# Paged attention: VectorE turns half of the latent columns in 32 by 32 blocks, scored on sixteen tiles

## The chip, the cores and the metric

The kernel runs on one core of one Trainium2 chip. The metric is the device time of one execution in microseconds (us). A profiled execution gives a span (first to last instruction) and a trace of every engine: PE (TensorE matmuls), PEld (its weight loads), VectorE (DVE), ScalarE (ACT), GpSimd (POOL) and SyncE (SP).

## What is computed

The reference is one step of a decoder layer for a prompt of 512 tokens and for 8 sequences with 4 new tokens each, over a paged cache of 4096 past positions per sequence. The part that matters here is the attention of the new tokens (8 heads, 32 queries per sequence in all) over the cache, in which each position is a row of 256 latent and 32 rope numbers:

```python
past = cache_l[page_table].reshape(Bd, -1, KV_CACHE_DIM)
q_lat = jnp.einsum('bthd,chd->bthc', q_nope, lp["w_uk"])          # absorption
s_past = einsum('bthc,bkc->bhtk', q_lat, pc) + einsum('bthr,bkr->bhtk', q_rope, pr)
p = softmax(concat(s_past, masked s_new) * MLA_SCALE)
ctx = einsum('bhtk,bkc->bthc', p[..., :n_past], pc) + einsum(..., p[..., n_past:], nc)
```

In front of it stands causal attention over the prompt (8 heads, blocks of 128 queries), behind it the output projection, cross-attention to a memory and an MLP. All of it is f32; the large projections are done as three fp32r products of high and low parts.

## The kernel before

Every engine has a program of its own, ordered by hand; semaphores tie them together. Stages, on PE: projections (`act_tile`, L582), prompt attention (L870 to L916), the paged loop (L976 to L999), then output projection, memory attention and MLP.

**Prompt attention** is a software pipeline over n = 0 to 36 (32 pairs of head and query block): PE makes the score of n (L885), VectorE adds the causal mask and takes the maximum (L1943, L1944), ScalarE the exp (L1518), VectorE scales by the reciprocal (L1949, L1950), PE turns p of n - 3 (L893), ScalarE copies it (L1526), PE multiplies by the values of n - 5 (L907). Between these, `k_pair` (three times inside the loop, at n = 3, 11, 17) makes two heads' keys. The **absorption** runs in the gaps: `absorb_turn` (n = 18, 20, 22, 24; L839) transposes w_uk, ScalarE copies it (L1537), `absorb` (n = 27, L847) makes 16 products of a 64 by 128 weight with 32 columns, VectorE copies the result into `qlat` by head (L1928). `new_rows` (n = 30, L858 to L863) scores the new tokens' own rows, with three waits of PE on itself between products of different tiling. VectorE spreads the rope queries into `qropez` (L1918), block-diagonal, which POOL has set to zero (L540).

**The paged loop.** One turn handles 2048 positions (half of a sequence), 16 in all. POOL gathers them by indirect DMA into one of four buffers `pg` (L526), 128 partitions by 16 positions by 288 numbers, as soon as the values of four turns ago are done. PE's order in turn n is `turn(n+1)`, `turn_p(n)`, `score(n+1)`, `values(n)`:

- `turn` (L929): 32 transposes of 128 by 128, four to a PSUM bank, four banks of `gps` in rotation; ScalarE (L1549) and VectorE (L1965) copy the banks alternately to `cT`.
- `score`: with the queries' latents as weights of 32 columns, on four column tiles (32j), 8 products of 512 columns (L943) and 16 rope products of 128 columns against `qropez` (L949), into `aux` bank 1 or 2.
- VectorE takes the maximum (L1981) and its negative (L1982), turns the rope part of the next page in 32 by 32 blocks (L1970); ScalarE makes exp with the sum (L1562).
- `turn_p` (L960): four transposes of p, copied by VectorE to `pTs` (L1990). `values` (L970): 16 products of 256 columns on four column tiles into `aux` bank 3, kept by ScalarE (L1553).

POOL's queue in this stage: the zeroing of `qropez` behind the last key tile, `gather(1)` behind the last `absorb_turn`, `gather(2)` behind `absorb`, `gather(3)` behind the last `at_lo`, then `gather(i+4)` behind `values(i)`; the split of the output weights stands behind all of them. The loop on PE:

```python
for n in range(NH - 1):
    turn(n + 1); turn_p(n); score(n + 1); values(n)
```

## Time and profile before

| | us |
|---|---|
| median of 3 runs | 1029.64 (1028.56 to 1030.25) |
| profiled execution: its own time | 1030.06 |
| its span | 1028.3 |
| busy: PE / PEld / VectorE / ScalarE / POOL | 996.3 / 900.5 / 515.4 / 300.4 / 447.5 |
| prompt attention, first score to first page transpose | 203.8 to 265.8 |
| paged loop, first turn with copies done to last exp | 274.8 to 402.5 |

The span is the stretch between the first and last instruction; 1.8 us of the execution lie around it. PE's ends are modelled, so a busy PE is one with work in its pipeline; start-to-start times tell what an instruction costs.

### The profile page before, as it was taken

What the parts mean: (1) busy time and instruction counts of PE and PEld (TensorE: products, weight loads), DVE (VectorE), ACT (ScalarE), POOL (GpSimd) and SP (SyncE); (2) the same over time, 40 slices, a digit from 0 to 9 for tenths busy, and PEclk for the clock granted to TensorE, in tenths of its full rate; (3) what the DMA queues carried; (4) which work ended last, traced back from release to release, by engine and by line L of the source; (5) the groups of instructions that cost most, each with busy time, mean ns of one, the idle gap of its engine ahead of it and who ended that gap; (6) DMA issues with size and microseconds to landing.
All of it is one profiled execution on the core that took longest, in us unless ns stands there. A gap on an engine that the chain in (4) does not pass through costs nothing.

```text
span 1028.3 us, 19824 instructions
## 1 busy us (share of the span) xinstructions
PE 996.3 (97%) x8517; PEld 900.5 (88%) x8517; DVE 515.4 (50%) x723; ACT 300.4 (29%) x602; POOL 447.5 (44%) x284
## 2 busy tenths in 40 slices
PE   5999999999999999999999999999999999999997
PEld 5989898766677777999965799999999999999997
DVE  5789998377455555563255366421341134114413
ACT  7333265475344443121035122210120022002222
POOL 4545688500011112555320155555555555555551
PEclk9999999998999999999999999999999999999998
DMA  7323365503377772822192022233223322332222
GB/s 227 84 67 81 104 184 153 169 32 152 147 274 278 278 279 80 270 83 82 61 404 90 21 83 83 82 94 92 82 83 91 94 83 83 93 93 83 83 82 87
DMA packets 140556, 130.39 MB, mean 127 GB/s; under 512 B 13477, under 2 KB 133170, under 8 KB 136630
## 3 DMA queue, kind: packets, MB, share of 16 engines
q1 hardware_dynamic: 134888, 88.55, 28.4%
q0 software_dynamic: 2304, 37.75, 9.5%
q10 hardware_dynamic: 3278, 2.83, 0.8%
q8 instruction: 67, 1.10, 0.4%
q14 instruction: 19, 0.16, 0.0%
HBM read 123.53 MB, written 5.03 MB: 125 GB/s over the span
## 4 chain that ended last, share of the span: by engine, by line
PE 84%; DVE 8%; ACT 2%; POOL 2%; DMA 2%; issue 2%; SPq 0%; ACTq 0%; DVEq 0%; POOLq 0%
PE gps L582 56%; PE gps L929 5%; PE aux L943 3%; PE aux L970 3%; PE aux L885 1%; PE gps L1085 1%; PE gps L1167 1%; PE aux L949 1%; PE gps L907 1%; POOL wlo L521 1%; PE gps L736 1%; PE gps L1005 1%; DVE act_lo L1681 1%; PE gps L718 1%; PE aux L1098 1%
## 5 line engine op out<-in xcount | busy, mean ns | idle before, releaser
L582 PE MATMUL gps<-act_hi,whi 128*128 128x272 f32 x912 | 265.8, 291 | 5.8 <-POOL wlo L511 3.4
L497 POOL TENSOR_SCALAR whi<-wraw 128x1024 fp32r<-128x1024 f32 (+1 forms) x109 | 114.6, 1052 | 360.1 <-PE gps L582 298.8
L582 PE MATMUL gps<-act_lo,whi 128*128 128x272 f32 x912 | 264.2, 290 | 0.0
L582 PE MATMUL gps<-act_hi,wlo 128*128 128x272 f32 x912 | 263.8, 289 | 0.0
L500 POOL TENSOR_TENSOR wlo<-wraw,whi 128x1024 fp32r<-128x1024 f32 (+1 forms) x109 | 257.5, 2363 | 9.1
L582 PE MATMUL gps<-h_hi,whi 128*128 128x272 f32 x640 | 185.7, 290 | 0.0
L582 PE MATMUL gps<-h_lo,whi 128*128 128x272 f32 x640 | 185.1, 289 | 0.0
L582 PE MATMUL gps<-h_hi,wlo 128*128 128x272 f32 x640 | 184.6, 288 | 0.0
L582 PEld LDWEIGHTS gps<-act_hi,whi 128*128 128x128 f32 x912 | 172.4, 189 | 6.9 <-issue 3.9
L582 PEld LDWEIGHTS gps<-act_hi,wlo 128*128 128x128 f32 x912 | 172.4, 189 | 0.3 <-issue 0.2
L582 PEld LDWEIGHTS gps<-act_lo,whi 128*128 128x128 f32 x912 | 172.3, 189 | 0.0
L2024 DVE TENSOR_TENSOR XT<-gps,XT 128x544 f32<-128x544 f32 x48 | 34.8, 724 | 174.3 <-PE gps L582 171.7
L582 PEld LDWEIGHTS gps<-h_hi,whi 128*128 128x128 f32 x640 | 120.5, 188 | 0.4
L582 PEld LDWEIGHTS gps<-h_hi,wlo 128*128 128x128 f32 x640 | 120.5, 188 | 0.1
L582 PEld LDWEIGHTS gps<-h_lo,whi 128*128 128x128 f32 x640 | 120.4, 188 | 0.0
L1630 ACT ACTIVATE ms<-mr 128x544 f32<-128x544 f32 x32 | 21.1, 660 | 287.2 <-DVE mr L2105 287.2
L2111 DVE TENSOR_TENSOR act_lo<-ms,act_hi 128x544 fp32r<-128x544 f32 x29 | 58.5, 2017 | 40.8 <-ACT act_hi L1634 40.8
L526 POOL DMA_INDIRECT pg<-in_cache_mla_dram,idx x16 | 15.2, 953 | 134.0 <-PE aux L970 99.2
L929 PEld LDWEIGHTS gps<-ident,pg 128*128 128x128 f32 x512 | 55.5, 141 | 8.1 <-issue 5.9
L929 PE MATMUL gps<-ident,pg 128*128 128x128 f32 x512 | 60.0, 275 | 1.1 <-DVE ctxn L1978 0.8
L1965 DVE COPY cT<-gps 128x512 f32<-128x512 f32 x64 | 44.1, 690 | 25.9 <-PE gps L929 25.8
L2105 DVE SCALAR_TENSOR_TENSOR mr<-gps,rsn 128x544 f32<-128x544 f32 x32 | 23.2, 725 | 65.4 <-PE gps L582 64.6
(367 smaller groups left out, 1539.0 us busy)
## 6 DMA issues: line engine op xcount, KB each, us to landing
wraw<-in_w_up_dram SPq DMA_DIRECT2D x32, 512.0 KB, 4.0
wraw<-in_w_down_dram SPq DMA_DIRECT2D x32, 512.0 KB, 3.7
wraw<-in_w_in_dram SPq DMA_DIRECT2D x14, 512.0 KB, 4.2
kv<-in_cache_mem_k_dram SPq DMA_DIRECT2D x7, 1024.0 KB, 7.0
kv<-in_cache_mem_v_dram SPq DMA_DIRECT2D x7, 1024.0 KB, 13.0
wraw<-in_w_mem_k_dram SPq DMA_DIRECT2D x16, 256.0 KB, 2.9
wraw<-in_w_mem_v_dram SPq DMA_DIRECT2D x16, 256.0 KB, 3.2
wraw<-in_w_out_dram SPq DMA_DIRECT2D x8, 512.0 KB, 4.7
```

The costliest lines, as they stand in the source:

```text
L497: nc.gpsimd.tensor_scalar(whi[:, slot, 0:n], wraw[:, slot, 0:n], 1.0, 1.0, ALU.mult, ALU.mult).then_inc(pool_step, 1)
L500: nc.gpsimd.tensor_tensor(wlo[:, slot, 0:n], wraw[:, slot, 0:n], whi[:, slot, 0:n].bitcast(F32), ALU.subtract).then_inc(w_ready, 1)
L526: nc.gpsimd.indirect_dma_start(pg[n % 4][:, :, :].rearrange("p k d -> p (k d)"), None, rows_of_pages, bass.IndirectOffsetOnAxis(ap=idx[:, ...
L582: mm = nc.tensor.matmul(out_of(a), w_of(w, k), x_of(x, k, part), start=(k == 0 and s == 0), stop=(k == k_tiles - 1 and s == 2))
L929: mm = nc.tensor.transpose(gps[:, (k + 1) % 4, 128 * z:128 * z + 128], pg[n % 4][:, 4 * j + z, 128 * c:128 * c + 128], ident[:, :])
L943: nc.tensor.matmul(out[32 * j:32 * j + 32, :], qlat[:, c, b, :], cT[:, c, 512 * j:512 * j + 512], start=(c == 0), stop=False, skip_group_c ...
L970: mm = nc.tensor.matmul(aux[32 * j:32 * j + 32, 3, 0:256], pTs[:, 128 * i + 32 * j:128 * i + 32 * j + 32], pg[n % 4][:, 4 * j + i, 0:CR], ...
L1630: nc.scalar.activation(ms[:, n % 2, :], mr[:, n % 2, :], ACT.Square).then_inc(mlp_sq, 1)
L1965: V.tensor_copy(cT[:, i // 4, 512 * (i % 4):512 * (i % 4) + 512], gps[:, (k + 1) % 4, :]).then_inc(g_td, 1)
L2024: step(V.tensor_tensor(x, gps[:, 2 * (t % 2):2 * (t % 2) + 2, 0:HALF], x, ALU.add))
L2105: V.scalar_tensor_tensor(out=halves(mr[:, n % 2, :]), in0=gps[:, 2 * (t % 2):2 * (t % 2) + 2, 0:HALF], scalar=0.0, in1=halves(rsn[:, :]), ...
L2111: V.tensor_tensor(hidden(n)[1], ms[:, n % 2, :], hidden(n)[0].bitcast(F32), ALU.subtract).then_inc(mlp_lo, 1)
```

## The change

- Of a page's 256 latent columns, PE transposes the first 128 only, in two parts (`turn(n, part)`), through two banks of `aux`, all copied by ScalarE. The other 128 VectorE turns in 32 by 32 blocks, four stream transposes per page straight from `pg` to `cB`, with no PSUM between.
- Within such a block only 32 latent numbers lie on 32 partitions, so the second half and the rope are scored as 5 x 4 x 4 products of 32 rows, 32 columns of weights and 128 moving columns, on all sixteen tiles, each row group into its own bank of `gps`. The first half is added by 16 products on four column tiles. Scores have one set of banks, read by one reduce and one exp over four banks. `qropez` is replaced by `qB` (the second half's queries, in four blocks of 32) and `qrope4`.
- `values(n-1)` stands between the two parts of `turn(n+1)`.
- The absorption is turned: w_uk's transposes stand at the start of prompt attention and are copied by VectorE; the product has q as the weights (32 columns) and w_uk as 256 moving columns; its result is copied, spread four times and transposed back in three rounds (`absorb_back`, `block_back`). `new_rows` takes rope and mask in one product of 96 rows, without waits on itself.
- POOL's zeroing goes; `gather(2)` waits for the last round of turning back.

```diff
-        qropez = at("qropez", [128, BD, 128], F32, M0 + 46016)
+        qB = at("qB", [128, BD, 4, 32], F32, M0 + 46016)
+        qrope4 = at("qrope4", [128, BD, 32], F32, M0 + 39936)
...
-                    nc.gpsimd.memset(qropez[:, :, :], 0.0).then_inc(pool_set, 1)
                     pool.wait_ge(wk_T, 4)
                     gather(1)
-                    pool.wait_ge(ql_ps, 1)
+                    pool.wait_ge(ql_ps, 4)
...
             def absorb_turn(g):
 
-                if g == 0:
-                    pe.wait_ge(tile_free[1], (T_UK + 3) // 2 + 1)
-                else:
-                    pe.wait_ge(wk_ev, g)
+                if g >= 2:
+                    pe.wait_ge(wk_ev, 2)
                 for i in range(4):
                     h, c = 2 * g + i // 2, i % 2
                     o = 512 * c + 64 * h
-                    mm = nc.tensor.transpose(W_BANK[0:64, 128 * i:128 * i + 128], wraw[:, U_UK % 2, o:o + 64], ident[:, :])
+                    mm = nc.tensor.transpose(gps[0:64, (1, 3, 2, 3)[g], 128 * i:128 * i + 128],
+                                             wraw[:, U_UK % 2, o:o + 64], ident[:, :])
                 mm.then_inc(wk_T, 1)
 
             def absorb():
 
                 pe.wait_ge(wk_ev, 4)
-                for h in range(H):
-                    for c in range(2):
-                        mm = nc.tensor.matmul(W_BANK[:, (c * H + h) * TS:(c * H + h + 1) * TS],
-                                              wukT[:, h, 128 * c:128 * c + 128], q[0:64, h, TP:T],
-                                              start=True, stop=True)
+                pe.wait_ge(tile_free[1], (T_UK + 3) // 2 + 1)
+                for g in range(2):
+                    for h in range(4):
+                        mm = nc.tensor.matmul(W_BANK[32 * h:32 * h + 32, CR * g:CR * g + CR], q[0:64, 4 * g + h, TP:T],
+                                              wukT[:, 4 * g + h, :], start=True, stop=True, skip_group_check=True)
                 mm.then_inc(ql_ps, 1)
 
+            def absorb_back():
+
+                pe.wait_ge(ql_ok, 1)
+                for c in range(2):
+                    for g in range(2):
+                        o = 256 * c + 128 * g
+                        mm = nc.tensor.transpose(W_BANK[:, o:o + 128], qln[:, g, 128 * c:128 * c + 128], ident[:, :])
+                mm.then_inc(ql_ps, 1)
+
+            def block_back(p):
+
+                pe.wait_ge(ql_ok, 2 + p)
+                for x in range(2):
+                    for g in range(2):
+                        o = 256 * x + 128 * g
+                        mm = nc.tensor.transpose(W_BANK[:, o:o + 128],
+                                                 qlr[:, g, 2 * p + x, :, :].rearrange("p r d -> p (r d)"), ident[:, :])
+                mm.then_inc(ql_ps, 1)
+
...
-                    nc.tensor.matmul(out, qrc[64:96, 128 * g:128 * g + 128], kr[64:96, TP:T], start=False, stop=False
-                                     ).then_inc(new_row, 1)
-                    pe.wait_ge(new_row, 2 * g + 1)
-                    mm = nc.tensor.matmul(out, newmask[0:TS, 4 * g:4 * g + 4, :].rearrange("p b q -> p (b q)"),
-                                          ident[0:TS, 0:TS], start=False, stop=True)
-                    if g == 0:
-                        mm.then_inc(new_row, 1)
-                        pe.wait_ge(new_row, 2)
+                    mm = nc.tensor.matmul(out, qrc[0:96, 128 * g:128 * g + 128], kr[0:96, TP:T], start=False, stop=True)
...
+            absorb_turn(0)
+            absorb_turn(1)
...
-                    if n in (3, 11, 17):
-                        k_pair(n // 8 + 1)
+                    if n == 3:
+                        absorb_turn(2)
+                        absorb_turn(3)
+                    if n == 4:
+                        pe.wait_ge(wk_ev, 3)
+                        k_pair(1)
+                    if n in (11, 15):
+                        k_pair((n + 1) // 5)
...
-                if 18 <= n <= 24 and n % 2 == 0:
-                    absorb_turn((n - 18) // 2)
-                if n == 27:
+                if n == 18:
                     absorb()
+                if n == 22:
+                    absorb_back()
+                if n in (25, 28):
+                    block_back((n - 25) // 3)
                 if n == 30:
...
-            def turn(n):
-
-                pe.wait_ge(page_in[n % 4], 16 * (n // 4) + 16)
-                for i in range(8):
-                    k = 8 * n + i
-                    if k >= 4:
-                        pe.wait_ge((g_ta, g_td)[k % 2], (k - 4) // 2 + 1)
+            def turn(n, part):
+
+                if part == 0:
+                    pe.wait_ge(page_in[n % 4], 16 * (n // 4) + 16)
+                for i in (2 * part, 2 * part + 1):
+                    k = 4 * n + i
+                    if k >= 2:
+                        pe.wait_ge(g_ta, k - 1)
                     else:
-                        pe.wait_ge((at_pT, new_act, at_lo, at_lo)[k], (4 * H, 2, 3, 4)[k])
+                        pe.wait_ge(at_exp, 4 * H)
                     for z in range(4):
-                        c, j = divmod(i, 4)
-                        mm = nc.tensor.transpose(gps[:, (k + 1) % 4, 128 * z:128 * z + 128],
-                                                 pg[n % 4][:, 4 * j + z, 128 * c:128 * c + 128], ident[:, :])
+                        mm = nc.tensor.transpose(aux[:, 1 + k % 2, 128 * z:128 * z + 128],
+                                                 pg[n % 4][:, 4 * i + z, 0:128], ident[:, :])
                     mm.then_inc(g_T, 1)
 
             def score(n):
 
                 b = n // 2
-                out = aux[:, 1 + n % 2, :]
-                if n >= 2:
-                    pe.wait_ge(g_exp, n - 1)
-                for c in range(2):
-                    for j in range(4):
-                        k = 8 * n + 4 * c + j
-                        pe.wait_ge((g_ta, g_td)[k % 2], k // 2 + 1)
-                        nc.tensor.matmul(out[32 * j:32 * j + 32, :], qlat[:, c, b, :],
-                                         cT[:, c, 512 * j:512 * j + 512], start=(c == 0), stop=False,
-                                         skip_group_check=True)
+                if n == 0:
+                    pe.wait_ge(at_pT, 4 * H)
+                    pe.wait_ge(new_act, 2)
+                    pe.wait_ge(at_lo, 4)
                 pe.wait_ge(g_rope, n + 1)
+                pe.wait_ge(g_td, 4 * n + 4)
+                for x in range(5):
+                    for g in range(4):
+                        rows = slice(32 * g, 32 * g + 32)
+                        for j in range(4):
+                            q_x, k_x = ((qB[rows, b, x, :], cB[rows, 4 * j:4 * j + 4, 32 * x:32 * x + 32]) if x < 4
+                                        else (qrope4[rows, b, :], ropT[rows, 4 * j:4 * j + 4, :]))
+                            nc.tensor.matmul(gps[32 * j:32 * j + 32, g, 0:128], q_x, k_x, start=(x == 0), stop=False,
+                                             skip_group_check=True)
+                pe.wait_ge(g_ta, 4 * n + 4)
                 for g in range(4):
                     for j in range(4):
                         mm = nc.tensor.matmul(
-                            out[32 * j:32 * j + 32, :].rearrange("p (i g k) -> p g i k", i=4, g=4)[:, g, :, :],
-                            qropez[:, b, 32 * g:32 * g + 32], ropT[:, 4 * j:4 * j + 4, :], start=False, stop=(g == 3),
-                            skip_group_check=True)
+                            gps[32 * j:32 * j + 32, g, 0:128], qlat[:, 0, b, :],
+                            cT[:, 512 * j:512 * j + 512].rearrange("p (i g k) -> p g i k", i=4, g=4)[:, g, :, :],
+                            start=False, stop=True, skip_group_check=True)
                 mm.then_inc(g_S, 1)
 
...
-                turn(n + 1)
+                turn(n + 1, 0)
+                if n:
+                    values(n - 1)
+                turn(n + 1, 1)
                 turn_p(n)
                 score(n + 1)
-                values(n)
...
-            def turned(n):
-                for k in range(8 * n, 8 * n + 8, 2):
+            def turned(n, part):
+                for k in (4 * n + 2 * part, 4 * n + 2 * part + 1):
                     act.wait_ge(g_T, k + 1)
-                    i = k % 8
-                    nc.scalar.copy(cT[:, i // 4, 512 * (i % 4):512 * (i % 4) + 512], gps[:, (k + 1) % 4, :]).then_inc(g_ta, 1)
+                    nc.scalar.copy(cT[:, 512 * (k % 4):512 * (k % 4) + 512], aux[:, 1 + k % 2, :]).then_inc(g_ta, 1)
 
...
-                nc.scalar.activation(ps[n % 2][:, :], aux[:, 1 + n % 2, :], ACT.Exp, bias=nm[:, n:n + 1],
-                                     scale=1.0, accum_out=sl[:, 1, n % 2, n // 2:n // 2 + 1]).then_inc(g_exp, 1)
+                nc.scalar.activation(ps[n % 2][:, :].rearrange("p (i g k) -> p g i k", i=4, g=4),
+                                     gps[:, :, 0:128].rearrange("p g (i k) -> p g i k", i=4), ACT.Exp,
+                                     bias=nm[:, n:n + 1], scale=1.0,
+                                     accum_out=sl[:, 1, n % 2, n // 2:n // 2 + 1]).then_inc(g_exp, 1)
+                if n < NH - 1:
+                    turned(n + 1, 0)
                 if n >= 1:
                     keep_ctx(n - 1)
                 if n < NH - 1:
-                    turned(n + 1)
+                    turned(n + 1, 1)
...
+            def spread(r):
+
+                src = gps[:, 2, :].rearrange("p (g c) -> p g c", g=2)[:, :, 128:256]
+                return V.tensor_copy(qlr[:, :, :, r, :], src.rearrange("p g (x d) -> p g x d", x=4))
+
+            def by_head(dst, x):
+
+                return V.tensor_copy(dst.rearrange("p b (h t) -> p h b t", t=TD),
+                                     gps[:, 2, x * 256:x * 256 + 256].rearrange("p (h b t) -> p h b t", h=H, t=TD))
+
             def absorbed(n):
 
                 if n == 18:
                     dve.wait_ge(tile_done, T_UK + 4)
-                    dve.wait_ge(pool_set, 9)
-                elif n < 23:
-                    if n == 19:
-                        dve.wait_ge(q_ok, 16 * H)
-                    r = 32 * (n - 19)
-                    step(V.tensor_copy(qropez[r:r + 32, :, r:r + 32].rearrange("p b (h t) -> p h b t", t=TD),
-                                       q[R, :, TP:T].rearrange("p h (b t) -> p h b t", t=TD)))
+                    dve.wait_ge(q_ok, 16 * H)
+                elif n == 19:
+                    dve.wait_ge(ql_ps, 1)
+                    V.tensor_copy(qln[:, :, :], gps[:, 2, :].rearrange("p (g c) -> p g c", g=2))
+                    spread(0)
+                elif n == 20:
+                    spread(1)
+                    spread(2)
+                elif n == 21:
+                    spread(3).then_inc(ql_ok, 1)
                 elif n == 23:
+                    dve.wait_ge(ql_ps, 2)
+                    by_head(qlat[:, 0, :, :], 0)
+                    by_head(qlat[:, 1, :, :], 1).then_inc(ql_ok, 1)
+                elif n in (26, 29):
+                    p = (n - 26) // 3
+                    dve.wait_ge(ql_ps, 3 + p)
+                    by_head(qB[:, :, 2 * p, :], 0)
+                    by_head(qB[:, :, 2 * p + 1, :], 1).then_inc(ql_ok, 1)
+                elif n == 24:
+                    V.memset(qrc[32:64, :], 0.0)
+                    V.memset(kr[32:64, TP:T], 0.0)
+                    V.tensor_copy(qrc[0:32, :].rearrange("p (b q) -> p b q", b=BD), newmask[:, :, :])
+                    V.tensor_copy(kr[0:32, TP:T], ident[0:32, 0:32])
                     step(V.tensor_copy(qrc[R, :].rearrange("p (b h t) -> p h b t", b=BD, t=TD),
                                        q[R, :, TP:T].rearrange("p h (b t) -> p h b t", t=TD)))
-                elif n == 24:
+                elif n == 27:
                     step(V.tensor_reduce(pick[:, :], ident[:, :].rearrange("p (j q) -> p q j", j=4), AX, ALU.add))
-                elif n == 28:
-                    dve.wait_ge(ql_ps, 1)
-                    for c in range(2):
-                        ins = V.tensor_copy(qlat[:, c, :, :].rearrange("p b (h t) -> p h b t", t=TD),
-                                            gps[:, 2, c * 256:c * 256 + 256].rearrange("p (h b t) -> p h b t", h=H, t=TD))
-                        if c == 0:
-                            step(ins)
-                    ins.then_inc(ql_ok, 1)
-                elif n == 32:
+                elif n == 31:
                     dve.wait_ge(new_pe, 1)
                     step(V.tensor_reduce(sn[:, 0, :], gps[:, 2, 0:64].rearrange("p (g k) -> p g k", g=2), AX, ALU.max))
                     V.tensor_scalar(nmn[:, :], sn[:, 0, :], -1.0, None, ALU.mult).then_inc(new_dve, 1)
-
+                elif n in (33, 34):
+                    for r in (64 * (n - 33), 64 * (n - 33) + 32):
+                        V.tensor_copy(qrope4[r:r + 32, :, :].rearrange("p b (h t) -> p h b t", t=TD),
+                                      q[R, :, TP:T].rearrange("p h (b t) -> p h b t", t=TD))
+
+            def turned_uk(g):
+
+                dve.wait_ge(wk_T, g + 1)
+                V.tensor_copy(wukT[:, 2 * g:2 * g + 2, :],
+                              gps[0:64, (1, 3, 2, 3)[g], :].rearrange("p (h n) -> p h n", h=2)).then_inc(wk_ev, 1)
+
+            turned_uk(0)
+            turned_uk(1)
...
+                if n == 2:
+                    turned_uk(2)
+                    turned_uk(3)
...
-                for k in range(8 * n + 1, 8 * n + 8, 2):
-                    dve.wait_ge(g_T, k + 1)
-                    i = k % 8
-                    V.tensor_copy(cT[:, i // 4, 512 * (i % 4):512 * (i % 4) + 512], gps[:, (k + 1) % 4, :]).then_inc(g_td, 1)
+                for j in range(0, 16, 4):
+                    V.transpose(cB[:, j:j + 4, :], pg[n % 4][:, j:j + 4, 128:256]).then_inc(g_td, 1)
...
-                step(V.tensor_reduce(sl[:, 0, n % 2, n // 2:n // 2 + 1], aux[:, 1 + n % 2, :], AX, ALU.max))
+                step(V.tensor_reduce(sl[:, 0, n % 2, n // 2:n // 2 + 1], gps[:, :, 0:128],
+                                     mybir.AxisListType.XY, ALU.max))
```

## Rows read from the trace of the kernel before

**Rows 1.** The page, the chain that ended last: shares of the span by engine.

```profile
PE 84%; DVE 8%; ACT 2%; POOL 2%; DMA 2%; issue 2%; SPq 0%; ACTq 0%; DVEq 0%; POOLq 0%
```

**Rows 2.** Windows: us, busy us (instructions) by engine, clock granted, DMA share, GB/s.

```profile
203.80:247.30 43.50, 39.77 (x270) 26.81 (x270) 35.23 (x114) 30.23 (x89) 1.90 (x2) 1.00 0.13 51
247.30:265.80 18.50, 18.16 (x118) 14.39 (x118) 8.06 (x28) 7.16 (x26) 0.94 (x1) 0.72 0.57 228
...
274.80:402.50 127.70, 127.51 (x1732) 93.35 (x1736) 72.98 (x122) 51.85 (x104) 14.97 (x15) 1.00 0.62 235
```

**Rows 3.** The chain through one turn of the loop: start us, us, what.

```profile
335.00 3.64 PE gps L929 x32
338.65 0.44 PE aux L960 x4
339.08 1.85 PE aux L943 x16
340.94 0.87 PE aux L949 x32
341.81 1.73 PE aux L970 x32
343.54 0.26 PE gps L929
```

**Rows 4.** Weight loads in the same turn, in order of time.

```profile
334.93 3.47 PEld L929 LDWEIGHTS gps<-ident,pg 128*128 128x128 f32 x32 [0.41 <-issue]
...
339.01 0.16 PEld L943 LDWEIGHTS aux<-cT,qlat 128*32 128x32 f32 x8 [0.17 <-issue]
```

**Rows 5.** Groups of instructions, 283.8 to 402.5: count, busy us, mean ns, idle before.

```profile
L1965 DVE COPY cT<-gps 128x512 f32<-128x512 f32 x56 | 38.7, 692 | 24.7 <-PE gps L929 24.7
L1549 ACT COPY cT<-gps 128x512 f32<-128x512 f32 x56 | 32.8, 586 | 14.6 <-PE gps L929 14.6
...
L1981 DVE TENSOR_REDUCE sl<-aux 128x1 f32<-128x512 f32 x14 | 9.7, 692 | 26.7 <-PE aux L949 26.7
L1990 DVE COPY pTs<-aux 128x512 f32<-128x512 f32 x14 | 9.5, 680 | 0.0
L1970 DVE STREAM_TRANSPOSE ropT<-pg 128x512 f32<-128x512 f32 x13 | 9.1, 701 | 0.0
L1562 ACT ACTIVATE ps<-aux,nm 128x512 f32<-128x512 f32 x13 | 8.9, 687 | 51.5 <-DVE nm L1982 51.5
...
L943 PEld LDWEIGHTS aux<-cT,qlat 128*32 128x32 f32 x224 | 5.8, 109 | 10.7 <-issue 10.7
```

**Rows 6.** PE at the query rope swap, on 32 by 32 tiles: start, us.

```profile
183.72 1.12 PE L776 MATMUL aux<-qr,swap 32*32 32x272 f32 x16
```

**Rows 7.** The page gathers: one issue on POOL's timeline, and all sixteen landings.

```profile
335.31 0.94 POOL L526 DMA_INDIRECT pg<-in_cache_mla_dram,idx  x1 [7.59 <-PE aux L970]
...
DMA to landing us min/median/max: 8.4/9.5/11.0
```

**Rows 8.** The page, DMA queues: packets, MB, share of 16 engines.

```profile
q0 software_dynamic: 2304, 37.75, 9.5%
```

**Rows 9.** The chain at the absorption, and VectorE before two later scores.

```profile
247.33 3.69 PE gps L847 x32
...
252.10 0.30 DVE L1943 TENSOR_TENSOR aux<-aux,causal 128x128 f32<-128x128 f32 x1 [3.06 <-PE aux L885]
...
261.36 0.30 DVE L1943 TENSOR_TENSOR aux<-aux,causal 128x128 f32<-128x128 f32 x1 [4.49 <-PE aux L885]
```

**Rows 10.** VectorE in prompt attention, 204.5 to 263.4, groups as in rows 5.

```profile
L1918 DVE COPY qropez<-q 32x256 f32<-32x256 f32 x4 | 1.1, 284 | 0.1
L1928 DVE COPY qlat<-gps 128x256 f32<-128x256 f32 x2 | 0.8, 421 | 0.0
```

**Rows 11.** Windows in late prompt attention, columns as in rows 2.

```profile
251.00:254.00 3.00, 3.00 (x12) 1.97 (x12) 1.80 (x6) 0.94 (x3) 0.94 (x1) 0.52 0.51 154
...
261.00:265.80 4.80, 4.63 (x36) 3.23 (x37) 2.20 (x9) 1.97 (x10) 0.00 (x0) 0.64 0.01 2
```

35 lines of the change are left out of this document (19 added, 16 removed).

## The prediction

> **What bounds the kernel now.** I read the chain that ended last first: 84% of it is TensorE [rows 1]. Then the windows by stage [rows 2]: prompt attention, 203.8 to 265.8 us, and the paged loop, 274.8 to 402.5 us, hold nearly all that the change touches. In the loop PE is busy in 127.51 of 127.70 us; in the first 43.5 us of prompt attention VectorE is busy in 35.23 and PE in 39.77. The rest of the kernel, projections and MLP, keeps its code.
>
> One turn of the loop [rows 3]: 32 transposes of the page 3.64 us, 4 of p 0.44, the latent score 1.85, the rope score 0.87, the values 1.73; sum 8.53, and the next turn begins at 343.54, 8.54 after 335.00. Nobody makes PE wait: the idle time in front of the copies on both helpers is put down to PE [rows 5]. So in the loop the time is PE's instruction list, 15 turns of 8.53.
>
> How small matmuls cost: each f32 matmul is two instructions. A transpose takes 3.64/32 = 0.114 with its share of a change of tiling; without it 0.109, the 0.44/4 of p's. The rope score, 16 matmuls of 128 columns on four column tiles, is 32 instructions in 0.87, 0.027 each: four run side by side, one wave per 0.109. Eight weight loads of four tiles fit into 0.16 us at 109 ns each [rows 4, 5], so loads follow each other by (0.16 - 0.109)/7 = 7 ns when their tiles are free. Sixteen tiles at 7 ns would be 0.11 us, just a wave.
>
> **The loop after.** PE per turn:
> 1. Page transposes: 16 instead of 32, 16 x 0.109 = 1.75 (saved 1.75).
> 2. p's four, unchanged, 0.44. Values, unchanged, 1.73.
> 3. First latent half: it was half of 1.85, 0.93; now 16 matmuls of 128 columns on four column tiles in four banks, the same form as the old rope score: 0.87.
> 4. Second half and rope: 80 matmuls of 32 by 32 with 128 columns, 160 instructions. The only 32-by-32 tiling with long streams is the query rope swap [rows 6]: 16 instructions of 272 columns in 1.12; a stream is 272/128 x 0.109 = 0.23, and four waves of four at 0.23 and the last one's drain fill just that: tiles that differ in row and column run together, but no row shows several row groups in one column group. The bounds: all sixteen in parallel, 10 waves x 0.109 = 1.09; row groups one after another, 40 x 0.109 = 4.37. I take 1.09: loads and matmuls of parked tiles are passed by others already (all four tiles start within 0.03 us although each tile's two passes stand together in the list), and the four banks keep the row groups' outputs apart. It replaces 0.93 + 0.87.
> 5. Changes of tiling. Two per turn show as gaps of the weight loads, 0.41 and 0.17 us [rows 4]; the delay in them is 8.53 less the streams, (32 + 4) x 0.109 + 16 x 0.109 (512 columns on four tiles) + 0.87 + 1.73, which leaves 0.26; I take 0.15 each. The new order (transposes, values, transposes, p, sixteen tiles, four tiles) has five: 0.75.
>
> Sum 1.75 + 0.44 + 1.73 + 0.87 + 1.09 + 0.75 = 6.63 us.
>
> Does another engine reach that? VectorE loses four copies of 0.69 and gains four stream transposes of 512 elements, 0.70 like the rope's [rows 5]: with reduce 0.69, negation 0.15, rope 0.70, p's copy 0.68 it has 5.0 of 6.6. Its order: reduce, negation, rope turn, four turns (about 4.2 after a score's end), while PE comes to the next score after 1.75 + 1.73 + 0.44 and four changes, 4.5. Near, but PE last. ScalarE keeps four copies of 0.59 and an exp. The single set of score banks is safe: reduce, negation and exp take 0.69 + 0.15 + 0.69 + 0.2, 1.8 with hand-overs, and PE has 3.9 of other work before it needs them. The p copy waits for p's transposes and hides beside the next score, since values now come a turn later.
>
> Pages: a gather takes 9.5 us from issue to landing, 0.94 of them on POOL [rows 7], and one turn's page is 37.75/16 = 2.36 MB; the queue's 9.5% of the span is 97.7/16 = 6.1 us a page with all sixteen DMA engines [rows 8]. So DMA alone allows 6.1. The gather of page n+4 waits for values n, which moved from the end of turn n to 2.9 us into turn n+1; with 0.5 for the hand-over (334.9 to the issue at 335.31) it lands 3.4 + 9.5 = 12.9 after that turn's start and is needed two turns on: a turn of 6.45 is allowed. Close below 6.63; for small waits where both are near I take **6.7**.
>
> Total of the stage: turn 0 has no values, but two of its copies stand behind the first exp: about 6.2. Then 14 x 6.7, and the last values outside the loop, 1.85: 101.9, against 15 x 8.53 = 128.0 and about 0.3 of first-turn waits. **Saved 26.4.**
>
> **Prompt attention.** The absorption was 32 instructions in 3.69 with VectorE idle 3.06 [rows 9]; turned it is 16 instructions of 256 columns on four tiles, 16/4 x 0.22 = 0.9. Three rounds of transposing back add 12 x 0.109 and six changes of tiling, 2.2. The new rows lose two mask products and the waits between them; VectorE waited 4.49 there; about 1.5 to 2 stays. Against that stands VectorE, which paces this part. Added inside it: two of the four weight copies moved from ScalarE (0.69; the first two lie before the first score, where it idles, but delay it by some 0.4), one 512 copy 0.69, four spreads and four more by-head copies at 0.42, the mask pieces for the joint product about 0.7, less four rope copies of 0.28 that go behind the last score [rows 10]: 1.3 + 0.7 + 3.4 + 0.7 - 1.1 + 0.4 = 5.4. Removed idle time: 2 + 2.7. ScalarE sheds 4 x 0.59, PE no longer stands for it in the weight turns. The clock fell to 0.52 at 251 and 0.64 in the last stretch [rows 11], each after sparse 32-column streams; losing one of these stretches gives back 1 to 2 us. Net: -0.5, between -5 and +4. The moved gathers (the second no longer behind the memset, the third behind the last turning back) have landed long before their turn; the waits on POOL's queue cost nothing, as the weight split behind them waits for the stage's end anyway. Start of the stage: the first score waits for VectorE's subtraction, rope turn and four turns, some 4.6 us, as it now starts 4.4 in: nothing.
>
> Sum against the profiled execution's 1030.06: - 26.4 - 0.5 = **1003**; it lies 0.4 above the median of 1029.64, which changes nothing.
>
> The Trainium skill, "TensorE: Matmul & The Clock Gate", Part 3, says that matmuls keep strict program order in start and end. By that rule, taken literally, the two passes of each of the 80 products would stand 0.109 apart one after the other: 8.7 us a turn and a kernel of over 1100. This trace disagrees already: 16 such products on four tiles take 0.87, not 1.75. The same page gives 10.6 times for sixteen tiles, which no row here shows.
>
> **Rivals.**
> - **A tile's second pass holds the next row group.** Within a column group the list reads first pass, second pass, next row group. If a column's queue stays in order, each of the 20 steps costs 0.109 + 0.007 to 0.027: 2.3 to 2.7, a turn of 7.85 to 8.25, the stage 119 to 125: 1020 to 1027, middle 1022. For it: no row has this case. Against: queues that let other tiles past. Chance 0.16. This is also the case that the tiling is not what it says.
> - **Gathers late.** Landing took up to 11.0 [rows 7]; now two are in flight. Then a turn is (3.4 + 11)/2 = 7.2, the stage 109: 1010. Chance 0.12.
> - **Row groups share a column's path.** The 160 instructions take 4.37, the turn 9.9: turn 0 9.5 + 14 x 9.9 + 1.85 = 150, 22 more: 1051. It decides against the change from 1.09 + 1.9 = 3.0 us for the 160. Chance 0.12.
> - Forecast, 0.6, its own range 997 to 1009.
>
> Numbers: 1003; the range 996 to 1023 leaves out the last rival and the upper end of the first. A measurement of this kernel tells 0.2%, 2 us, from no change. The top of the first rival with 2 or 3 us more in prompt attention is no change: faster 0.86, same 0.02, slower 0.12.
>
> **What would show it.** Loop turns of 6.6 to 6.8 in the chain, PE still without waits; the 160 small matmuls spanning about 1.1 us a turn. 2.3 to 2.7 or 4.4 there is the first or last rival; a wait of PE or VectorE for a page's DMA at turn starts is the second. VectorE waits of less than 2 us around absorption and new rows, prompt attention within 4 us of 62. Wrong altogether if the clock falls inside the loop, or if a change of tiling costs much more than 0.15.

## The result and the profile after

| | before | after |
|---|---|---|
| median of 4 runs, us | 1029.33 (1028.56 to 1030.25) | 1079.61 (1078.28 to 1082.92) |
| profiled span, us | 1028.3 | 1078.8 |
| first score of prompt attention to first page transpose | 62.0 | 59.5 |
| from there to the start of the loop | 9.0 | 12.4 |
| loop, 15 turns | 127.7 | 177.8 |
| from the loop's end to the end of the span | 625.8 | 625.6 |

The changed kernel is slower, 1.05 times the time of before (95% interval 1.0482 to 1.0518). The forecast was 1003 us, with a range of 996 to 1023. The table puts the whole loss into the loop: 50.1 of 50.5 us.

The windows of the changed kernel by stage: us, busy us (instructions) by engine, clock granted, DMA share, GB/s. They answer to [rows 2].

```profile
203.60:247.30 43.70, 39.64 (x265) 26.50 (x266) 34.69 (x109) 26.28 (x78) 0.94 (x1) 0.96 0.22 89
247.30:263.00 15.70, 13.02 (x108) 8.82 (x106) 13.86 (x50) 9.21 (x32) 0.94 (x1) 1.00 0.40 151
263.00:275.40 12.40, 8.31 (x216) 6.08 (x214) 4.78 (x10) 2.73 (x5) 0.94 (x1) 0.84 0.57 237
275.40:453.20 177.80, 139.02 (x3656) 101.14 (x3660) 68.64 (x122) 48.30 (x105) 18.00 (x16) 0.86 0.44 168
```

The last line is the loop. PE, busy without a break before, is busy in 139.02 of 177.80 us, and its clock, 1.00 before, is granted at 0.86 on average: part of the time it is at the lower of its two levels, 1.2 GHz instead of 2.4. No other engine is near its limit, and DMA moves less than before (168 GB/s for 235). The number of PE's instructions is in the same line: 3656 matmuls where the loop had 1732.

What does PE wait for? The waits of PE in the loop: what it stood in front of, the releaser, us in total, how often, the longest.

```profile
PE gps L975 <- issue: 17.7, 8, 4.9
PE gps L980 <- issue: 11.4, 3, 4.4
PE aux L1001 <- issue: 6.1, 3, 2.2
PE aux L956 <- issue: 3.3, 1, 3.3
```

"issue" means that no semaphore, engine or transfer known to the profile held it: 38.5 us of nothing. In the chain that ended last "issue" rose from 2% [rows 1] to 5%. The stops are long, few, and in four different places of the code (the small products, the first-half products, the values, the transposes), so they don't belong to one instruction. PE's timeline around one of them, start, us, what, idle before:

```profile
349.34 1.64 PE L975 MATMUL gps<-cB,qB 32*32 32x128 f32 x102
...
350.83 0.67 PE L975 MATMUL gps<-ropT,qrope 32*32 32x128 f32 x28
351.43 0.41 PE L980 MATMUL gps<-cT,qlat 128*32 128x128 f32 x5
355.55 0.87 PE L980 MATMUL gps<-cT,qlat 128*32 128x128 f32 x12 [3.70 <-issue]
```

The first line starts with the window; its group began at 349.18. PE stops after five of a row of 32 like instructions. Windows cut from one resumption to the next show the pattern:

```profile
316.60:341.00 24.40, 18.77 (x511) 13.29 (x511) 9.05 (x16) 6.38 (x14) 1.87 (x2) 0.85 0.52 198
341.00:355.60 14.60, 10.90 (x258) 7.62 (x261) 4.53 (x8) 3.19 (x7) 0.94 (x1) 0.73 0.42 161
355.60:370.30 14.70, 10.34 (x258) 7.60 (x261) 4.53 (x8) 3.19 (x7) 0.94 (x1) 0.85 0.43 165
```

About 256 matmuls and as many weight loads lie in each. Counted in the trace itself, with PE's semaphore instructions, it is 1024 instructions in the first window and 511 to 513 in each of the others, these two and the ones behind them: twice 256. The page has a DMA queue for instructions; its lines for the kernel before and, second, the changed one (packets, MB, share):

```profile
q8 instruction: 67, 1.10, 0.4%
```

```profile
q8 instruction: 83, 1.36, 0.5%
```

A packet is 16,384 bytes, 256 instructions of 64; I call these 256 a block. PE's 21,420 recorded instructions divided by 83 are 258: the queue feeds PE. In the records of the packets, each stop ends 1.2 to 1.6 us after one of them has landed. Every second block is on time, every second one is late, since a turn has two blocks (488 instructions and some waits, 232 before) and the sixteen-tile products run through most of one of them in 2 us:

```
changed kernel, counted from the stops in steps of 256 instructions
block entered   next packet runs      next block entered   PE idle before it
334.22          338.64 to 339.54      340.97               4.85
340.97          342.01 to 342.95      349.66               0
349.66          353.16 to 354.10      355.55               3.70
355.55          357.08 to 358.00      363.59               0
363.59          367.87 to 368.81      370.25               4.36
```

In the loop the packet mostly starts 0.8 to 1.9 us after a block is entered when the DMA engines are free, and 3.5 to 4.4 after it when a gather is running. The DMA share and the bytes of one gather, 333 to 342 us, in 40 slices (it was issued on POOL at 332.18):

```profile
DMA  0009970029939939937937977977991000100000
q0 software_dynamic: 144, 2.36, 68.7%
q8 instruction: 1, 0.02, 0.6%
```

One instruction packet among 128 gather packets of 18,432 bytes (and 16 small ones). That is theory F; the experiments try it.

It need not be a gather. The loop's last stop (4.14 us idle, ended at 448.66) follows the last gather: the block entered at 441.42 had its next packet only 4.73 us later, and 7.24 us passed to the next block. The DMA engines were busy with the output weights, in 2028 packets of some 510 bytes, 441.4 to 446.1 us:

```profile
q1 hardware_dynamic: 2028, 1.03, 78.0%
```

### The profile page after: what moved, and what is told of

It is laid out like the page before. It is cut to its first block, busy times and chain, and to the rows that moved or that the text cites. A ratio compares the mean times of both kernels' runs of the same rounds, so it can differ in the third digit from the quotient of the medians.

```text
span 1078.8 us, 23919 instructions
## 1 busy us (share of the span) xinstructions
PE 1001.2 (93%) x10557; PEld 902.0 (84%) x10557; DVE 516.9 (48%) x740; ACT 293.9 (27%) x598; POOL 446.0 (41%) x283
## 4 chain that ended last, share of the span: by engine, by line
PE 78%; DVE 9%; issue 5%; POOL 2%; ACT 2%; DMA 2%; SPq 0%; ACTq 0%; DVEq 0%; POOLq 0%
PE gps L584 53%; PE gps L975 4%; PE aux L956 3%; PE aux L1001 3%; PE gps L980 2%; PE gps L1119 1%; POOL wlo L524 1%; PE gps L1201 1%; PE gps L1040 1%; DVE act_lo L1714 1%; PE gps L720 1%; DVE sm L2007 1%; DMA wraw<-in_w_mem_v_dram 1%; PE aux L991 1%; PE aux L1132 1%
## 5 line engine op out<-in xcount | busy, mean ns | idle before, releaser
L524 POOL TENSOR_TENSOR wlo<-wraw,whi 128x512 fp32r<-128x512 f32 x32 | 48.8, 1557 | 12.9 <-ACT whi L1363 12.9
L2045 DVE TENSOR_REDUCE sl<-gps 128x1 f32<-128x512 f32 x16 | 11.1, 691 | 78.0 <-PE gps L980 78.0
L1714 DVE SCALAR_TENSOR_TENSOR h_lo<-XT,vec,h_hi 128x544 fp32r<-128x544 f32 x16 | 40.5, 2533 | 15.6 <-ACT h_hi L1293 15.6
```

Source lines behind the costliest of these rows:

```text
L524: ins = nc.gpsimd.tensor_tensor(wlo[:, slot, part], wraw[:, slot, part], whi[:, slot, part].bitcast(F32), ALU.subtract)
L1714: V.scalar_tensor_tensor(out=lo, in0=XT[:, k, :], scalar=cols(gain, k), in1=hi.bitcast(F32), op0=ALU.mult, op1=ALU.subtract).then_inc(nx_l ...
```

## The experiments

Theories: **F**, the instruction block comes late because its packet waits among the gather's. **R1**, it comes late by its own latency, now that a turn has twice the instructions. **R2**, the stops are the sixteen tiles' own. Except in the last experiment each kernel was run once; before, run beside them, took 1027.6 to 1029.6 us.

### No gathers in the loop (e1_four_gathers)

```diff
-                    for i in range(NH - 4):
-                        pool.wait_ge(g_V, i + 1)
-                        gather(i + 4)
```

> The changed kernel with only the first four page gathers of sixteen; the later row groups read the four page buffers again, so what is computed for them is wrong data at the same cost. Theory F (TensorE stands still at every second block of 256 instructions, because the block's fetch, a 16,384 B packet, is queued on a DMA engine behind the gather's 18,432 B packets): the 2 to 5 us gaps of the loop disappear as soon as no gather runs, the granted clock of the loop stays near 1.0, a turn takes 7.2 to 8.2 us, and the kernel 1010 to 1032 us. Rival R1 (the fetch is late by its own latency, since a turn now has twice the instructions; gathers don't matter): gaps stay, 1065 to 1080 us. Rival R2 (the gaps are the sixteen-tile products' own, no matter of fetches): gaps stay, 1065 to 1080 us.

Measured: 1034.42 us. The loop, and two windows between resumptions:

```profile
299.40:308.70 9.30, 7.89 (x254) 5.85 (x254) 4.53 (x8) 3.19 (x7) 0.00 (x0) 1.00 0.01 4
308.70:318.00 9.30, 9.29 (x254) 7.00 (x254) 4.53 (x8) 3.19 (x7) 0.00 (x0) 0.82 0.02 4
265.40:404.90 139.50, 124.29 (x3812) 93.76 (x3816) 69.60 (x124) 47.57 (x104) 0.13 (x1) 0.96 0.08 29
```

And one stop, on PE's timeline:

```profile
306.99 0.30 PE L972 MATMUL gps<-ropT,qrope 32*32 32x128 f32 x3
308.71 0.71 PE L972 MATMUL gps<-ropT,qrope 32*32 32x128 f32 x25 [1.43 <-issue]
```

45 of the 50 us are gone with the gathers, so most of it is F. But the stops did not disappear, they shrank to 1.84 us and less, again 512 instructions apart: R1 holds for the rest. With idle DMA engines the packet typically starts 1.0 us after a block is entered, ends at 2.0 and opens the next block at some 3.4 us (2.9 to 3.5 in seven cases, 4.1 and 4.7 in two). A block that PE runs through faster than that stops it in any case. A turn is 139.5/15 = 9.3 us, still above before's 8.53, and above the 7.2 to 8.2 that F gave; the time, too, is 2 us over F's range.

The kernel before with the same lines removed is the control.

> The kernel before with only the first four gathers of sixteen (later row groups compute on old pages). Theory F: its 232 instructions a turn need one block of 256 in over 8 us, more than the 6.7 us that a fetch beside a gather took at most in the changed kernel, so that nothing is gained: 1025 to 1031 us, and no gaps in the loop. If the gathers cost the loop something else (TensorE reading more slowly beside them), it is faster by more than that: 1020 us or less.

Measured: 1028.83 us, before beside it 1027.58. The gathers cost it nothing.

### Twice the instructions in the kernel before (e4_before_split, e5_before_split_four_gathers)

```diff
-                        nc.tensor.matmul(out[32 * j:32 * j + 32, :], qlat[:, c, b, :],
+                        for s in range(4):
+                            nc.tensor.matmul(out[32 * j:32 * j + 32, 128 * s:128 * s + 128], qlat[:, c, b, :],
...
-                        mm = nc.tensor.matmul(aux[32 * j:32 * j + 32, 3, 0:256],
+                        for s in (0, 128):
+                            mm = nc.tensor.matmul(aux[32 * j:32 * j + 32, 3, s:s + 128],
```

The rope products are cut in two in the same way. The pieces begin their sums in a bank that others have begun, so the sums are not the reference's.

> The kernel before with its first score products cut into four of 128 columns, its rope products into two of 64 and its value products into two of 128: the same columns and the same four tiles, but 228 pairs of instructions a turn where it has 116, near the changed kernel's 244. Theories F and R1 (instruction fetch): gaps of 2 to 5 us appear in a kernel without sixteen tiles, they end 512 instructions apart, the turn grows by the 112 small pairs (some 1.5 us) and by the gaps (some 3 us), 1070 to 1105 us. Rival R2 (the gaps belong to sixteen tiles): no gaps, only the pairs: 1035 to 1055 us.

> The split kernel of the run before it, with only the first four gathers of sixteen (later row groups compute on old pages). Theory F: no gaps any more, the small pairs' own time is left: 1035 to 1055 us. R1: like the split kernel with all gathers, gaps included, within 10 us.

Measured: 1068.86 with all gathers, 1066.43 with four. The loop with all gathers, PE's only waits for "issue" in it, and then the loop with four:

```profile
274.00:438.00 164.00, 162.50 (x3274) 155.85 (x3276) 72.09 (x120) 51.80 (x104) 14.03 (x14) 1.00 0.48 182
```

```profile
PE aux L973 <- issue: 1.3, 3, 0.6
```

```profile
274.00:438.00 164.00, 163.34 (x3373) 157.81 (x3377) 72.69 (x122) 51.80 (x104) 5.21 (x4) 1.00 0.03 9
```

The first time lies between what was expected of F and R1 (1070 and more) and of R2 (1055 at most), and the stops of 2 to 5 us did not come: a kernel with nearly the changed kernel's count has three short ones and no more. The second is near the first, the number that R1 gave, but not for its reason, as there are no stops in it. The 40 us are the 112 extra pairs' own time: 39.6/16 = 2.5 us a turn, 22 ns a pair. The count alone is harmless because it is spread: from one block of 256 to the next pass mostly 4.4 to 9 us, and where it is less (2.7 to 3.3, three times) the packet came early. What counts is how fast a block is used up.

### Fewer small products (e3_two_of_five, e15_three_of_five)

```diff
-                for x in range(5):
+                for x in (0, 4):
```

> The changed kernel with only 32 of its 80 small score products (the second, third and fourth 32 latent columns of the second half are left out of the scores; VectorE still turns them): 296 instructions a turn instead of 488, still in sixteen tiles. Theory F: 1.2 blocks a turn at some 6.3 us beside a gather are 7.4 us, so hardly a gap is left and the turn is 7.5 to 8.1 us: 1018 to 1035 us. R2 (the gaps belong to sixteen tiles, whose products are still there): at most the time of the products left out is saved, 1.2 us a turn: 1055 to 1065 us.

> The changed kernel with 48 of its 80 small score products (the third and fourth 32 latent columns of the second half are left out of the scores): 360 instructions a turn, between the 296 of the run with 32 products and the 488 of the whole. Theory F (time goes by the number of blocks of 256 instructions): 1.45 blocks a turn at some 6.4 us are 9.3 us a turn, kernel 1035 to 1052 us. A share of the products' own time alone (0.4 us for each 32 columns): 1060 us or more; if the loss needs all five rounds of products (a matter of one burst's length): 1010 to 1018 us.

Measured: 1007.03 with 32 small products a turn, 1024.86 with 48, 1079.6 with 80. The loop with 32, and its "issue" waits:

```profile
265.00:380.00 115.00, 107.47 (x2339) 76.13 (x2339) 71.84 (x129) 49.23 (x109) 13.51 (x15) 0.96 0.74 283
```

```profile
PE aux L1001 <- issue: 2.3, 2, 1.6
PE gps L980 <- issue: 1.2, 2, 0.8
```

R2 falls: sixteen tiles are there in both, and a turn takes 7.0 us (first small product of the second turn to that of the last, over 14). Both runs came out below what F gave. I had put every block at 6.3 us; blocks entered outside a gather are faster, so the loss grows more steeply than the count. 16 products of 13 ns a pair are 0.4 us a turn, 6.6 us in all; the first sixteen left out bring some 27 us each (54.7 for two), the next 17.8. The difference is the stops and the clock.

### One pass instead of two (e8_single_pass)

```diff
+                            q_x, k_x = (a.bitcast(mybir.dt.bfloat16) for a in (q_x, k_x))
-                            nc.tensor.matmul(gps[32 * j:32 * j + 32, g, 0:128], q_x, k_x, start=(x == 0), stop=False,
+                            nc.tensor.matmul(gps[32 * j:32 * j + 32, g, 0:128], q_x[:, 1::2], k_x[:, :, 1::2], start=(x == 0), stop=False,
```

> The changed kernel with its small score products on the upper halves of the same numbers (read as 16-bit floats, so less exact), which makes one pair of instructions of each product instead of two: 80 products in the same sixteen tiles, 328 instructions a turn instead of 488. Theory F: 1.3 blocks a turn at some 6.3 us are 8.1 us, the turn is 7.6 to 8.6 us and the kernel 1020 to 1045 us, with shorter and fewer gaps. R2: 16-tile gaps stay, only the 1 us of the halved products goes: 1060 us or more.

Measured: 1016.47 us. All 80 products in all sixteen tiles, at half their instructions: 11 us faster than before, and again a few us below what F gave. R2 is out for good. It is no version to keep, as it scores half of the latent columns and the rope from 16 bits. Stops remain, up to 2.9 us (9.5 us in front of the values), and from one block to the next beside a gather passed 5.8 to 7.0 us.

### Smaller packets, and gathers at another time

The gather in four (or two) parts reads a quarter (half) of each row's bytes, with an index table for each part:

```diff
+                for s in range(4):
                     nc.gpsimd.indirect_dma_start(
-                    pg[n % 4][:, :, :].rearrange("p k d -> p (k d)"), None, rows_of_pages,
-                    bass.IndirectOffsetOnAxis(ap=idx[:, n:n + 1], axis=0)).then_inc(page_in[n % 4], 16)
+                        pg[n % 4][:, 4 * s:4 * s + 4, :].rearrange("p k d -> p (k d)"), None, rows_of_parts,
+                        bass.IndirectOffsetOnAxis(ap=idp[:, s, n:n + 1], axis=0)).then_inc(page_in[n % 4], 16)
```

> The changed kernel with every gather cut into four of a quarter of the bytes each (4,608 B a packet instead of 18,432), everything computed as before. F, if the fetch waits for packets that are already under way or takes turns with the gather's: smaller packets let it in sooner, gaps shrink by half or more, 1030 to 1055 us. F, if the whole backlog of the gather on that DMA engine is ahead of the fetch: gaps stay as the bytes do, 1070 to 1085 us. R1 and R2: no change, 1075 to 1085 us. GpSimd issues four times as many gathers; if their preparation takes long, pages come late and the turn grows, 1085 us or more.

Measured: 1062.79 us, 17 us better than the whole gathers. The late blocks beside a gather now took 4.1 to 6.3 us, most of them 5.3 or less, where they took 5.8 to 6.7. The packet gets in sooner. That it is the size of the gather's packets that lets it in is not shown by this: the four issues are also spread, 1.25 us apart.

> The changed kernel with every gather in two of half the bytes (9,216 B a packet). Theory F with the fetch taking its turn among the gather's packets: between the whole gather (1079.6 us) and the quarters (1062.8 us), 1064 to 1075 us, with block times between 6.5 and 4.6 us. If the quarters had gained by something other than the size of a packet (when they start), it is at one end or the other.

Measured: 1081.91 us, no gain at all: late blocks of 5.7 to 6.6 us but for one, and two new pauses, of some 0.3 and 0.56 us, inside the small products of most turns. That is the upper end of the second case, so packet size alone does not explain what the quarters gained; neither would it explain the 4.73 us beside packets of 510 bytes.

A gather issued behind the small products:

```diff
                         pool.wait_ge(g_V, i + 1)
+                        pool.wait_ge(g_S, i + 3)
```

> The changed kernel with every gather from the fifth on issued behind the small score products of the turn instead of ahead of them (one wait more on GpSimd; everything computed as before). Theory F: the block whose instructions run fastest, that of the small products, is then fetched with the DMA engines free (3.4 us from the block before to it, as in the run with four gathers), only the other one of a turn lies beside the gather (some 6.5 us): 9.9 us a turn where it was 10.9, kernel 1050 to 1068 us; if the gathers only slide until they meet the next dense block again, 1070 to 1082 us. If the gaps have to do with how late the pages come, it gets slower: 1085 us or more.

Measured: 1070.52 us, at the lower edge of the second case; eight stops of 2.2 to 4.4 us were left and had slid to other places of the turn, and PE waited twice for a page, 6.7 us in all. Both together:

> Both together: quarters, and issued behind the small products. Theory F: the dense block is fetched in some 3.4 us, the other in some 4.6 us, and the small products no longer run beside GpSimd's four issues (they took 2.6 us where they take 2.05 otherwise): 1035 to 1052 us. If the position of the gather doesn't matter: 1060 to 1065 us, as with the quarters alone.

Measured: 1077.56 us, a miss: worse than the quarters alone. PE waits for pages here too, 6.0 us.

> The single-pass kernel with every gather in four of a quarter of the bytes (4,608 B a packet). Theory F: both cures together, 1.3 blocks a turn at 4.6 us are 6.0 us, so the fetches are hidden and the gathers' own 7.6 us a page or TensorE's work bounds the turn: 1010 to 1028 us, at or below the kernel before. Otherwise within 5 us of the single-pass kernel.

Measured: 1070.3 us, the plainest miss of the study, 54 us above the same kernel with whole gathers. PE's groups in its loop:

```profile
L978 PE MATMUL gps<-cB,qB 32*32 32x128 bf16 x1024 | 26.9, 230 | 37.7 <-issue 35.7 <-DVE cB L2035 1.9
```

And one turn's small products on PE's timeline:

```profile
333.40 0.54 PE L978 MATMUL gps<-cB,qB 32*32 32x128 bf16 x41
334.36 0.26 PE L978 MATMUL gps<-cB,qB 32*32 32x128 bf16 x5 [0.42 <-issue]
335.09 0.27 PE L978 MATMUL gps<-cB,qB 32*32 32x128 bf16 x6 [0.46 <-issue]
336.52 0.26 PE L978 MATMUL gps<-cB,qB 32*32 32x128 bf16 x4 [1.16 <-issue]
```

These are not block ends: starts stand 0.68 us or twice that apart, and the 80 products take 4.7 us instead of 0.65 in twelve of the sixteen turns, all of them with a divided gather being issued.

> The single-pass kernel with quarters, issued behind the small products. In the same kernel with the issues ahead, the 80 small products took 4.7 us a turn instead of 0.65, in pauses of 0.68 us, while GpSimd prepared its four gathers. Theory P (the preparation of a gather on GpSimd holds up the small products): they take 0.65 us again, 1005 to 1020 us. Rival (the running gather's small packets hold them up, whenever they were issued, or where the data lie): they still take over 3 us in most turns, 1050 to 1075 us.

Measured: 1047.08 us. The 80 products take 0.65 us in nine of sixteen turns and 1.4 to 2.8 in seven; in addition PE now waits for pages, which start too late:

```profile
L959 PE MATMUL aux<-ident,pg 128*128 128x128 f32 x248 | 41.0, 318 | 20.6 <-DMA pg<-in_cache_mla_dram,idp 19.4 <-DVE ctxn L2049 0.8 <-ACT cT L1581 0.4
```

Neither side's numbers were met. What makes the 0.68 us pauses stays open: they came only with divided gathers, and moving the issues away thinned them without ending them. The f32 products with quarters have no such pause, but in the turns without a stop they take 2.5 to 3.0 us, mostly 2.6, instead of 2.05.

### The other part of the change alone (e14_prompt_part)

The kernel before with the new prompt attention, minus what only the new loop needs; the four rope copies write `qropez` as before:

```diff
-                if 18 <= n <= 24 and n % 2 == 0:
-                    absorb_turn((n - 18) // 2)
-                if n == 27:
+                if n == 18:
                     absorb()
+                if n == 22:
+                    absorb_back()
```

> The kernel before with only the other part of the change: the absorption turned (weights ahead of the prompt attention, queries as the stationary side, one masked product for the new rows), the loop over the pages as before; everything computed. In the changed kernel's trace the loop's first transpose came 0.7 us later than before, so if the loop is the whole loss this is 1028 to 1031 us, within 0.2% of before. Rival R3 (the turned absorption costs time that the loop's gaps hid, for example through later gathers or a clock that falls again): 1033 us or more. My forecast on record (half a microsecond gained): 1028.5 to 1029.2 us.

Measured: 1024.21 us (median of 7 runs, 1023.3 to 1025.92), before 1029.62 (10 runs); ratio 0.9943, 95% interval 0.9923 to 0.9964. That is below every case written down for it. It computes all of the reference and is faster than both kernels. Its windows, from the first score (202.91 on its timeline) on, to be held against [rows 2]:

```profile
202.80:246.00 43.20, 39.31 (x269) 25.57 (x267) 34.61 (x110) 27.31 (x81) 2.83 (x3) 1.00 0.29 110
...
259.80:268.80 9.00, 8.13 (x88) 5.70 (x86) 5.02 (x10) 2.92 (x5) 0.94 (x1) 1.00 0.74 286
268.80:396.50 127.70, 127.50 (x1732) 93.34 (x1736) 73.03 (x122) 51.79 (x104) 14.92 (x15) 1.00 0.62 234
```

And the end of its prompt attention beside before's, on windows of a few us:

```profile
250.00:256.00 6.00, 5.24 (x44) 4.03 (x45) 4.45 (x16) 4.49 (x13) 0.00 (x0) 1.00 0.00 0
256.00:260.00 4.00, 3.34 (x39) 2.47 (x39) 3.33 (x13) 2.03 (x11) 0.00 (x0) 1.00 0.03 6
```

```profile
250.00:256.00 6.00, 6.00 (x30) 4.73 (x30) 3.39 (x11) 1.63 (x6) 0.94 (x1) 0.59 0.72 273
256.00:262.00 6.00, 5.83 (x39) 4.40 (x37) 1.41 (x7) 1.77 (x5) 0.00 (x0) 0.78 0.56 236
```

The loop and the nine us ahead of it are before's to a tenth. The gain lies ahead: the first page transpose comes at 259.82, 56.9 us after the first score, where before has 62.0. The granted clock may tell nearly all of it: 0.59 and 0.78 behind the old absorption, when PE had run its 32-column products, and 1.00 here. Over before's whole 62.0 us it is 0.92, 5.0 us of clock withheld, against none here; the gain is 5.1. No run parts the clock from the shorter waits of VectorE. The changed kernel had 59.5 (no run explains its 2.6 us more), and it lost its gain again at once: its first score waited 1.87 us for `cB`, an instruction block was late for 1.2 us, and the stretch to the loop took 12.4 us instead of 9.0.

## Why the prediction was wrong

**The step that failed is that PE's time in the loop is PE's instruction list alone.** The sum priced 488 instructions a turn by what each occupies and none by what it takes to bring them. The trace of before held the warning: 67 instruction packets, one per 256 instructions, that is one per 9 us of loop or so, beside gathers that keep the DMA engines busy for most of a turn. 488 instructions in the forecast 6.7 us need a block every 3.5 us, and 320 of them run in 2 us, so that a block inside them lasts 1.6 us; the chip opened the next one after some 3.4 us with idle DMA engines and after 5.8 to 6.7 beside a gather. None of the rivals named it, and the range ended 57 us too low. By the profile PE's stops are 38.5 us. The clock comes next: it fell behind stops, and the same instructions then took longer. As an estimate, 0.14 of 177.8 us are 25 us of clock withheld, and 15 turns of 7.6 us (below) are 114: 114 + 38.5 + 25 = 177.5 is near the loop's 177.8 (some of the 25 lies inside the stops, so the fit is in part luck), and a gain of 14 us turned into a loss of 50. PE's groups in the loop, changed kernel first, then with four gathers:

```profile
L1001 PE MATMUL aux<-pg,pTs 128*32 128x256 f32 x476 | 35.6, 434 | 6.1 <-issue 6.1
...
L980 PE MATMUL gps<-cT,qlat 128*32 128x128 f32 x480 | 21.9, 327 | 11.4 <-issue 11.4
```

```profile
L998 PE MATMUL aux<-pg,pTs 128*32 128x256 f32 x448 | 27.4, 382 | 0.0
L977 PE MATMUL gps<-cT,qlat 128*32 128x128 f32 x500 | 19.6, 295 | 3.0 <-issue 3.0
```

"Wrong altogether if the clock falls inside the loop" stood in the text; it fell, as a consequence and not as the cause: with the gathers gone and the stops short, the loop's clock is 0.96.

The Trainium skill, "Runtime: NRT & Kernel Launch", Instruction fetch mechanics, says that instructions come in 16 KiB blocks of 256 through a DMA queue of the sequencer's own, the next one while the current one runs. On the size and on one block ahead this trace agrees (packets of 16,384 bytes, 511 to 513 instructions between resumptions, and each packet starts after the block before it has been entered). It also says that fetching is hidden because an engine issues more slowly than blocks arrive; here the measurement decides against that: 38.5 us of stops.

**The turn's terms,** against the chain of a turn whose stop was short (start us, us, what):

```profile
325.12 2.12 PE gps L975 x115
327.23 0.30 issue
327.53 0.45 PE gps L975 x15
327.98 1.01 PE gps L980 x32
328.99 1.02 PE aux L956 x8
330.01 1.86 PE aux L1001 x32
331.88 1.02 PE aux L956 x8
332.90 0.44 PE aux L991 x4
```

- First half 1.01, values 1.86, p 0.44: as forecast (0.87, 1.73 and 0.44, with 0.15 for the tiling). Transposes 2.04 for 1.75 and two changes: right.
- The 160 small passes were mis-sized: without a stop their starts span 2.05 us (from 349.18 on), 13 ns each on average, and the next group starts 2.25 us after the first, instead of 1.09. The pace is not even. The first 32 passes start 7 ns apart, as I took from eight weight loads; from the second round of sixteen products on, each round of 32 passes takes 0.434 us, four streams of 0.109, although a tile has only two of them. The issue alone doesn't ask for that: with 16-bit numbers a round of 16 passes takes 0.133 us, 8.3 ns each, and 32 of these would be 0.27. Even without any fetch problem the turn would be 2.25 + 1.01 + 1.86 + 0.44 + 2.04 = 7.6 us, and the kernel some 14 us faster than before, not 26.
- The rival of row groups sharing a path (4.37) is out. The one of the second pass (2.3 to 2.7 in 20 steps of 0.109 and more) fits the pace of the later rounds, four steps of 0.109 each, but not the first round, which is faster. I gave it 0.16; no run tries it further.
- The Trainium skill, "TensorE: Matmul & The Clock Gate", Part 3, says that matmuls keep program order in start and end. The prediction made more of this than it says: order alone doesn't make products on different tiles wait for each other, so the 8.7 us a turn don't follow from it. But the order of the starts is not what this trace shows either. The rope's products stand behind all of the second half's in the list, and start among them:

```profile
350.74 0.29 PE L975 MATMUL gps<-ropT,qrope 32*32 32x128 f32 x1
350.75 0.32 PE L975 MATMUL gps<-cB,qB 32*32 32x128 f32 x4
```

- Late gathers: out. No engine waits for a page's DMA in the loop; PE did for 0.5 us in all with 32 small products, and for 6.0 to 19.4 in the three kernels where the gathers were moved on purpose.
- VectorE's order: right in the loop, as PE never waits for `cB` there; wrong for the first score, where the turning of the first page came 1.87 us late.

**Prompt attention** was forecast at -0.5, between -5 and +4. Alone, with the loop as before, it is worth -5.4 (1029.62 to 1024.21), just outside that. Two terms were mis-sized. I had given "1 to 2 us" for the stretches at half clock, where before's windows have 5.0 us of clock withheld and the new ones none; how much of the 5.4 us this made is not shown. And I added 5.4 us of VectorE's work as if it stood on the path, where VectorE's busy time from the first score to the first page transpose rose by 2.7 us (43.29 to 45.96).

## What to carry to other kernels

Beside what an instruction costs, count instructions: a block of 256 that PE ran through in less than the time of a fetch (some 3.4 us here) stopped it, and other DMA traffic in flight, of large packets or of small ones, about doubled that time; in a profile this is "issue" idle time at equal distances of instructions, and the instruction queue's packets tell how often it can happen. Many small tiles were fast here only in bursts shorter than a block, so a gain from them should be reckoned with a possible stop per block. And take the parts of a change apart: here one part, worth 0.6%, was hidden behind the other's loss of 5%.

## What the runs showed that I had not expected

- When PE waits for it, an instruction block opens some 3.4 us after the one before it with idle DMA engines, 5.8 to 6.7 beside a gather in packets of 18,432 bytes, 4.1 to 6.3 beside one in packets of 4,608 bytes, 7.24 beside weight loads in packets of 510 bytes. From the packet's end to the first instruction it is 1.2 to 1.6 us.
- Sixteen 32 by 32 tiles run side by side, row groups of one column group too: f32 passes of 128 columns start 13 ns apart on average, in rounds of 32 per 0.434 us, 16-bit products 8 ns (80 in 0.65 us). Their starts are not in the order of the list.
- With gathers in four, 16-bit small products pause in steps of 0.68 to 0.72 us or twice that, up to 4 us a turn; with gathers in two, f32 ones pause for some 0.3 and 0.56 us. No run settles why.
